# Sample attentions in four 32-column tiles, with contiguous cache runs, in a one-core decoder layer

## The chip, the core and the metric

The program runs on one core of a Trainium2 chip. Its engines are PE (TensorE, matmuls), DVE (VectorE), ACT (ScalarE), POOL (GpSimd) and SP (SyncE, which computes nothing and issues most of the transfers). The metric is the device time of one execution in microseconds (us). All data is fp32. The profile shows an fp32 matmul as two records on PE, each with a weight load of its own on PEld; a transpose, which is a matmul against the identity, is one record.

## What is computed

The layer takes a prompt of 1024 tokens and 8 samples of 8 new tokens each. The two parts that the change touches belong to the samples. In the self attention a sample has a cache of 1024 positions with 8 heads of 64; in the cross attention it has 256 memory positions with 4 heads of 256. Cut to what matters:

```python
# self attention of a sample, per dilation group (window, dil); kk, vv = cache + new rows
idx = wb + t[:, None] - kidx[None, :] * dil
s = einsum('bthd,btkhd->bthk', q, kk[idx]) * Dh ** -0.5 - slope * kidx * dil
o = einsum('bthk,btkhd->bthd', exp(s - lse), vv[idx])      # groups merged by their denominators
# cross attention of a sample
s = einsum('bthd,bmhd->bhtm', q, cache_mem_k) * 256 ** -0.5
o = einsum('bhtm,bmhd->bthd', softmax(s), cache_mem_v)
```

The kernel merges the three dilation groups into one softmax: a bias table holds the penalty and the logarithm of how many groups hold a key. The order of the keys is free as long as keys, values and bias agree on it.

## The kernel before

The kernel is a list of phases. In each, every engine has its own code, and between phases PE, DVE, ACT and POOL meet at a barrier (`meet`), so a phase that ends earlier moves all that follows. SP runs through its transfers with waits on semaphores and is not held by the barrier except where it waits for a phase by name. Nothing schedules the work: the order on an engine is the order of the code.

**Phase "win", the self attention over the cache** (`win_load`, `win_tensor`, `win_scalar`, `win_vector`). The keys of a sample (2 MB) and its values (2 MB) each have two buffers, `kc` and `vc`. Position `t * 128 + p` lies in partition p, so a partition receives eight runs of 2 KB. SP loads both in one queue: a key load waits until the transposes of the sample two before are done, a value load until that buffer's values have been used; the first two value loads wait until the stores of the phase before have landed. PE turns the keys (`turn_k(b, p)`, L1315: for each of four head pairs p eight transposes, four into bank 0 that ACT copies out and four into bank 1 that DVE copies out, `take_k`, L1391, into `kT`), and takes the scores of sample b from `kT` (`scores`, L1329). The stationary operand `QX[:, p, b, :]` has 64 columns (8 heads x 8 tokens) with zeros for the heads outside the pair p; four matmuls over p accumulate each of the two 512-key chunks and the 64 new keys. An even sample fills output rows 0 to 63, an odd one rows 64 to 127. `turn_k` of the next sample is spread between the pairs. Per pair of samples DVE and ACT do one softmax on 128 rows x 1088 (`softmax`, L1433 to L1441, with the exponential on ACT, L1417); `turn_p` turns the weights into `wpt`; `values` (L1360) multiplies them with all 512 value columns, eight cached blocks and one of new values per sample, 64 output rows at a time; of the result each head uses only its own 64 columns. `take_values` copies bank 7 out, `turn_o` turns it, and `output` (L1451) picks the useful blocks with 16 small copies. A `values` runs after the scores of every odd sample from the third on, for the pair before.

**Phase "xsample", the cross attention over the memory cache** (`xsample_load`, `xsample_tensor`, `xsample_scalar`, `xsample_vector`). Keys and values of a sample are 1 MB each. `turn_k(b, q)` (L1674) does four transposes into one of two banks and ACT copies them out (L1731). The scores of sample b (L1686) go to the 32-column tile `(0, 32 * i)` with i = b % 4: eight matmuls of 256 columns accumulate there, with a `turn_k` of the next sample after every second. After four samples (a quad) follow softmax, `values` (L1707: per sample four matmuls of 512 columns, all in the tile of that sample), the copy out (L1745), eight transposes (L1712) and the copies into `xhi` and `xlo`. SP loads the keys two samples ahead; the values of samples 0 to 3 are issued behind the keys of samples 0 and 1, those of 4 to 7 after all keys and once the buffer is free.

## Time and profile before

| what | value |
|---|---|
| median of three runs | 2445.07 us (2442.49 to 2447.41) |
| the profiled execution | 2447.53 us |
| its span in the trace | 2445.9 us |
| phase "win" | about 816 to 1005 us of the span |
| phase "xsample" | about 1404 to 1495 us of the span |
| PE busy, whole span | 2166.6 us (89%) |

The profile has a page with sums and the trace has the instructions with their start times. A time such as 904.90 is in us from the start of the span. The busy time of a matmul record includes its way through the array, so records that follow each other overlap in the trace; what PE needs per record is the distance between starts. "Idle before, releaser" names what an engine waited for; "issue" is time in which nothing visible held it.

### The profile page before, as it was taken

How to read it: one execution, taken by the hardware profiler on the slowest of the kernel's cores; microseconds unless marked ns; L12 is line 12 of the kernel's file. 1: busy time of each engine (PE TensorE's matmuls, PEld its weight loads, DVE VectorE, ACT ScalarE, POOL GpSimd, SP SyncE). 2: the span in 40 equal slices, each digit the busy share in tenths (PEclk: the TensorE clock that was granted, in tenths of full speed). 3: DMA queues.
4: the chain of work that ended last, by engine and by line, in shares of the span. 5: the costliest groups of instructions: out<-in, count | busy, mean ns of one | idle time of the engine just before them, and what ended most of it. 6: DMA issues, size and time to landing. Idle time of an engine off the chain costs nothing.

```text
span 2445.9 us, 29363 instructions
## 1 busy us (share of the span) xinstructions
PE 2166.6 (89%) x12542; PEld 1955.7 (80%) x12542; DVE 948.6 (39%) x1711; ACT 429.6 (18%) x759; POOL 70.2 (3%) x82
## 2 busy tenths in 40 slices
PE   6997997999377799498899788989999999999995
PEld 5995777999266544198898735989999999999995
DVE  7322442246665422444722301353333333333344
ACT  2004552001311121322201321030000000000013
POOL 3001000000021000000000000000000000000000
PEclk9998998999688799799999998999999999999997
DMA  5204331110053553311420042111111111111111
GB/s 174 61 17 168 130 121 36 43 43 17 15 190 138 181 200 120 138 56 45 138 69 35 4 181 99 43 43 43 32 54 44 39 40 51 43 41 52 41 30 73
DMA packets 181441, 188.94 MB, mean 77 GB/s; under 512 B 15879, under 2 KB 153639, under 8 KB 180586
## 3 DMA queue, kind: packets, MB, share of 16 engines
q1 hardware_dynamic: 180970, 170.97, 21.4%
q10 hardware_dynamic: 384, 16.78, 1.8%
q8 instruction: 59, 0.97, 0.2%
q14 instruction: 28, 0.23, 0.0%
HBM read 170.95 MB, written 50.33 MB: 90 GB/s over the span
## 4 chain that ended last, share of the span: by engine, by line
PE 47%; DVE 2%; ACT 2%; DMA 1%; issue 1%; DVEq 0%; ACTq 0%
PE psum L252 41%; PE psum L1560 1%; PE psum L1686 1%; PE psum L1707 1%; PE psum L1674 1%; ACT scratch L1581 1%; DVEq L182 0%; DMA weights_work<-in_cache_mem_k_dram 0%; DVE weights_lo L209 0%; DVE scratch L1618 0%; PE psum L1549 0%; DVE weights_hi L207 0%; PE psum L300 0%; DMA out_y_p_dram<-wide 0%; DMA weights_raw<-in_w_cv_dram 0%
## 5 line engine op out<-in xcount | busy, mean ns | idle before, releaser
L252 PE MATMUL psum<-x_hi,weights_hi 128*128 128x384 f32 (+1 forms) x2328 | 521.7, 332 | 43.5 <-DVE x_lo L290 18.9
L252 PE MATMUL psum<-x_lo,weights_hi 128*128 128x384 f32 (+1 forms) x2328 | 517.6, 330 | 0.0
L252 PE MATMUL psum<-x_hi,weights_lo 128*128 128x384 f32 (+1 forms) x2328 | 517.1, 330 | 0.0
L252 PEld LDWEIGHTS psum<-x_hi,weights_hi 128*128 128x128 f32 x2328 | 402.0, 190 | 49.1 <-issue 40.7
L207 DVE CAST weights_hi<-weights_raw 128x1024 fp32r<-128x1024 f32 (+2 forms) x144 | 94.6, 657 | 844.4 <-PE psum L252 830.8
L252 PEld LDWEIGHTS psum<-x_lo,weights_hi 128*128 128x128 f32 x2328 | 401.7, 190 | 0.0
L252 PEld LDWEIGHTS psum<-x_hi,weights_lo 128*128 128x128 f32 x2328 | 401.5, 189 | 0.0
L209 DVE TENSOR_TENSOR weights_lo<-weights_raw,weights_hi 128x1024 fp32r<-128x1024 f32 (+2 forms) x144 | 165.9, 1152 | 4.9
L252 PE MATMUL psum<-hidden_hi,weights_hi 128*128 128x384 f32 x528 | 117.2, 330 | 2.0 <-DVE hidden_lo L1822 2.0
L252 PE MATMUL psum<-hidden_lo,weights_hi 128*128 128x384 f32 x528 | 116.8, 329 | 0.0
L252 PE MATMUL psum<-hidden_hi,weights_lo 128*128 128x384 f32 x528 | 116.8, 329 | 0.0
L1795 ACT ACTIVATE scratch<-scratch 128x1088 f32<-128x1088 f32 x22 | 24.5, 1113 | 419.5 <-DVE scratch L1809 419.5
L252 PEld LDWEIGHTS psum<-hidden_hi,weights_hi 128*128 128x128 f32 x528 | 90.8, 189 | 2.2 <-DVE hidden_lo L1822 2.2
L252 PEld LDWEIGHTS psum<-hidden_lo,weights_hi 128*128 128x128 f32 x528 | 90.7, 189 | 0.0
L252 PEld LDWEIGHTS psum<-hidden_hi,weights_lo 128*128 128x128 f32 x528 | 90.6, 188 | 0.0
L567 PE MATMUL psum<-wide 128*128 128x512 f32 (+2 forms) x192 | 77.5, 514 | 1.9 <-ACTq L182 1.9
L618 DVE CUSTOM_DVE_ANT_0 scratch<-psum,weights_work 128x128 f32<-128x128 f32 (+3 forms) x64 | 48.5, 758 | 64.3 <-PE psum L567 41.6
L1797 ACT ACTIVATE hidden_hi<-scratch 128x1088 fp32r<-128x1088 f32 x22 | 24.5, 1114 | 269.0 <-DVE scratch L1820 269.0
L241 DVE TENSOR_TENSOR residual_T<-psum,residual_T 128x384 f32<-128x384 f32 x144 | 67.8, 527 | 5.7 <-PE psum L252 5.6
L579 PEld LDWEIGHTS psum<-ident,scratch 128*128 128x128 f32 x288 | 33.6, 142 | 43.1 <-ACT scratch L642 30.5
L1329 PE MATMUL psum<-wide,sample_q_wide 128*64 128x512 f32 x128 | 61.9, 607 | 4.4 <-DVE small L1438 2.7
L642 ACT ACTIVATE scratch<-scratch,small 128x128 f32<-128x128 f32 (+3 forms) x64 | 49.5, 774 | 92.1 <-DVE small L621 92.0
(295 smaller groups left out, 2245.5 us busy)
## 6 DMA issues: line engine op xcount, KB each, us to landing
work<-in_cache_win_k_dram SPq DMA_DIRECT2D x8, 2048.0 KB, 10.1
work<-in_cache_win_v_dram SPq DMA_DIRECT2D x8, 2048.0 KB, 9.7
weights_raw<-in_w_in_dram SPq DMA_DIRECT2D x28, 512.0 KB, 3.7
weights_raw<-in_w_gate_dram SPq DMA_DIRECT2D x22, 512.0 KB, 3.8
weights_raw<-in_w_up_dram SPq DMA_DIRECT2D x22, 512.0 KB, 3.7
weights_raw<-in_w_down_dram SPq DMA_DIRECT2D x24, 384.0 KB, 3.1
weights_work<-in_cache_mem_k_dram SPq DMA_DIRECT2D x8, 1024.0 KB, 5.0
wide<-in_cache_mem_v_dram SPq DMA_DIRECT2D x8, 1024.0 KB, 9.8
```

The lines of the kernel that those rows point to most:

```text
L207: nc.vector.tensor_copy(whi[:, w, 0:nk, :], raw[:, w, 0:nk, :]).then_inc(w_high, 1)
L209: nc.vector.tensor_tensor(wlo[:, w, 0:nk, :], raw[:, w, 0:nk, :], whi[:, w, 0:nk, :].bitcast(F32), ALU.subtract)\
L241: last = nc.vector.tensor_tensor(out, PS[:, 3 * ((n0 + j) % 2) + c, 0:w], out, ALU.add)
L252: mm = nc.tensor.matmul(PS[:, 3 * s + c, 0:n], w[:, s, k], x[part][:, k, t0:t0 + n], start=(k == 0 and w is whi and part == 0), stop=(k == ...
L567: mm = nc.tensor.matmul(PS[:, 2 * (u % 2) + g, 0:w], q_pad[:, h % 2, qb * P:(qb + 1) * P], ak[:, h // 2, 512 * g:512 * g + w], start=True, ...
L579: mm = nc.tensor.transpose(PS[:, 4 + n % 2, j * P:(j + 1) * P], logit[:, u % 3, (4 * g + j) * P:(4 * g + j + 1) * P], IDENT[:, :])
L618: chains["dve"](nc.vector.tensor_tensor_reduce(logit[:, u % 3, 0:w], PS[:, 2 * (u % 2):2 * (u % 2) + 2, :].rearrange("p a b -> p (a b)")[: ...
L642: nc.scalar.activation(logit[:, u % 3, 0:w], logit[:, u % 3, 0:w], ACT.Exp, bias=negm[:, i:i + 1], accum_out=asum[:, i:i + 1]).then_inc(pr ...
L1329: mm = nc.tensor.matmul(PS[HD * e:HD * e + HD, 2 + c, 0:w], QX[:, p, b, :], x, start=(p == 0), stop=(p == NP - 1))
L1560: mm = nc.tensor.matmul(PS[:, 6 + i // 4, (i % 4) * P:(i % 4 + 1) * P], mv_tok[:, m, i * P:(i + 1) * P], xpt[:, t % 2, (2 * h + m) * P:(2 ...
L1795: nc.scalar.activation(silu_g[:, q % 2], silu_g[:, q % 2], ACT.Silu).then_inc(silu_done, 1)
L1797: nc.scalar.activation(ghi[:, i], silu_g[:, q % 2], ACT.Copy).then_inc(h_high, 1)
```

## The change

Both sample attentions now spread each step over the four 32-column tiles of the array, with consecutive matmuls in different tiles.

- Self attention, scores: tile p holds head pair p, with 32 columns (2 samples x 2 heads x 8 tokens). `QX` has zeros for the other sample, and the two samples of a pair accumulate into the same rows. For each chunk of keys the four tiles take one matmul each. The transposes of the next sample follow the first chunk, the second chunk and, twice, the new keys.
- Self attention, values: tile p multiplies its 32 columns of weights with only the 128 value columns of its two heads. A sample has 36 matmuls of 128 columns where it had 9 of 512. The result is 256 columns wide for a pair of samples, so the copy out is half as wide, `turn_o` has two transposes for four, and `output` four copies for 16.
- Cross attention: tile h holds head h with the 32 rows of a quad. Scores of a sample are two groups of four matmuls, each followed by two `turn_k`; values are eight matmuls of 256 columns per sample.
- All four loads of cached keys and values give partition p the positions `p * n` to `p * n + n - 1`, one contiguous run of 16 KB (self) or 8 KB (cross). The bias table is permuted alike.
- The cached values of the self attention are issued by ACT, in `win_scalar`; SP keeps the keys, one after the other.

The core of the diff:

```diff
-        QX = sb("sample_q_wide", P, NP, DB, NS)
+        QX = sb("sample_q_wide", P, NP, DB, 32)
-                         A["cache_win_k"][b].rearrange("(t p) h d -> p t (h d)", p=P)).then_inc(kc_landed[b % 2], 16)
+                         A["cache_win_k"][b].rearrange("(p t) h d -> p t (h d)", p=P)).then_inc(kc_landed[b % 2], 16)
...
-            for pair in range(DB // 2):
-                if pair + 1 < DB // 2:
-                    load_k(sp, 2 * pair + 2)
-                if pair == 0:
-                    sp.wait_ge(out_stored, 16 * mark["state"])
-                    load_v(0)
-                    load_v(1)
-                if pair + 1 < DB // 2:
-                    load_k(sp, 2 * pair + 3)
-                if pair:
-                    load_v(2 * pair)
-                    load_v(2 * pair + 1)
+            for b in range(2, DB):
+                load_k(sp, b)
...
-                for p in range(NP):
-                    for c, (w, x) in enumerate(((512, k[:, p, 0:512]), (512, k[:, p, 512:PAST]), (NS, KNEW[:, p, :]))):
-                        mm = nc.tensor.matmul(PS[HD * e:HD * e + HD, 2 + c, 0:w], QX[:, p, b, :], x,
-                                              start=(p == 0), stop=(p == NP - 1))
-                    if p == NP - 1:
+                for c, w in enumerate((512, 512, NS)):
+                    for p in range(NP):
+                        x = KNEW[:, p, :] if c == 2 else k[:, p, 512 * c:512 * c + 512]
+                        mm = nc.tensor.matmul(PS[32 * p:32 * p + 32, 2 + c, 0:w], QX[:, p, b, :], x,
+                                              start=(e == 0), stop=(e == 1), tile_position=(0, 32 * p))
+                    if c == 2:
                         mm.then_inc(ws_ready, 1)
                     if b + 1 < DB:
-                        turn_k(b + 1, p)
+                        turn_k(b + 1, c)
+                if b + 1 < DB:
+                    turn_k(b + 1, 3)
...
-                    cs = slice(HD * e, HD * e + HD)
                     for t in range(KT + 1):
-                        p, v = (wpt[:, t, cs], vb[:, t, :]) if t < KT else (wpt[0:NS, t, cs], VNEW[:, :])
-                        mm = nc.tensor.matmul(PS[cs, 7, :], p, v, start=(t == 0), stop=(t == KT))
+                        for p in range(NP):
+                            rows = slice(32 * p, 32 * p + 32)
+                            w, v = (wpt[:, t, rows], vb[:, t, p * P:(p + 1) * P]) if t < KT else \
+                                (wpt[0:NS, t, rows], VNEW[:, p * P:(p + 1) * P])
+                            mm = nc.tensor.matmul(PS[rows, 7, e * P:(e + 1) * P], w, v, start=(t == 0), stop=(t == KT),
+                                                  tile_position=(0, 32 * p))
...
                 if b + 1 < DB:
                     take_k(act, 0, b + 1)
+                if b == 0:
+                    act.wait_ge(out_stored, 16 * mark["state"])
+                    load_v(act, 0)
+                    load_v(act, 1)
...
                     nc.scalar.activation(wl[:, :], wl[:, :], ACT.Exp, bias=negm[:, 0:1], accum_out=asum[:, 0:1]).then_inc(wl_free, 1)
+                    if b >= 3:
+                        act.wait_ge(wo_ready, b - 2)
+                        load_v(act, b - 1)
+                        act.wait_ge(wo_ready, b - 1)
+                        load_v(act, b)
...
-                    for k in range(KB):
-                        mm = nc.tensor.matmul(PS[32 * i:32 * i + 32, 2, 0:NMEM], cqx[:, k, b, :], ckT[b % 2][:, k, :],
-                                              start=(k == 0), stop=(k == KB - 1), tile_position=(0, 32 * i))
+                    for half in range(2):
+                        for h in range(XH):
+                            mm = nc.tensor.matmul(PS[32 * h:32 * h + 32, 2, 0:NMEM], cqx[:, 2 * h + half, b, :],
+                                                  ckT[b % 2][:, 2 * h + half, :], start=(i == 0 and half == 0),
+                                                  stop=(i == 3 and half == 1), tile_position=(0, 32 * h))
...
-                        if k % 2 and b + 1 < DB:
-                            turn_k(b + 1, k // 2)
+                        if b + 1 < DB:
+                            turn_k(b + 1, 2 * half)
+                            turn_k(b + 1, 2 * half + 1)
...
-                    for half in range(2):
-                        for m in range(2):
-                            mm = nc.tensor.matmul(PS[rows, 4 + half, :], ypt[:, m, rows], vb[:, m, 512 * half:512 * half + 512],
-                                                  start=(m == 0), stop=(m == 1), tile_position=(0, 32 * i))
+                    c0 = (i % 2) * XD
+                    for m in range(2):
+                        for h in range(XH):
+                            rows = slice(32 * h, 32 * h + 32)
+                            mm = nc.tensor.matmul(PS[rows, 4 + i // 2, c0:c0 + XD], ypt[:, m, rows], vb[:, m, h * XD:(h + 1) * XD],
+                                                  start=(m == 0), stop=(m == 1), tile_position=(0, 32 * h))
```

What stands in a row on the engines changes at three places. PE in the phase "win", from the first transposes on (L1315 is now L1305, L1329 now L1320; `128x128` is a transpose, the shape is output rows x moving columns). Before:

```order
L1315 MATMUL psum<-ident,work_55 128x128 x32
L1329 MATMUL psum<-wide,sample_q_wide 64x512 x2
L1329 MATMUL psum<-sample_k_new,sample_q_wide 64x64
L1315 MATMUL psum<-ident,work_55 128x128 x8
L1329 MATMUL psum<-wide,sample_q_wide 64x512 x2
```

After:

```order
L1305 MATMUL psum<-ident,work_55 128x128 x32
L1320 MATMUL psum<-wide,sample_q_wide 32x512 x4
L1305 MATMUL psum<-ident,work_55 128x128 x8
L1320 MATMUL psum<-wide,sample_q_wide 32x512 x4
L1305 MATMUL psum<-ident,work_55 128x128 x8
L1320 MATMUL psum<-sample_k_new,sample_q_wide 32x64 x4
L1305 MATMUL psum<-ident,work_55 128x128 x16
```

A sample had four alternations of scores and transposes; it has three, with the last 16 transposes in a row.

PE at the values of one pair in the same phase (L1360 is now L1355). Before:

```order
L1360 MATMUL psum<-work_54,scratch 64x512 x8
L1360 MATMUL psum<-sample_v_new,scratch 64x512
```

After:

```order
L1355 MATMUL psum<-work_54,scratch 32x128 x32
L1355 MATMUL psum<-sample_v_new,scratch 32x128 x4
L1355 MATMUL psum<-work_54,scratch 32x128 x32
```

Each sample has four times as many matmuls, each a quarter as long in moving columns.

ACT in the same phase, where the value loads (`work_54`) now stand among its copies and exponentials (L1391 is now L1387). After, from the start of the phase:

```order
L1387 ACTIVATE wide<-psum 128x512 x8
L1292 DMA work_54<-in_cache_win_v_dram 128x4096 x2
L1387 ACTIVATE wide<-psum 128x512 x4
L1417 ACTIVATE scratch,small<-scratch,small 128x1088
L1387 ACTIVATE wide<-psum 128x512 x4
L1398 ACTIVATE scratch<-psum 128x512 x2
L1400 ACTIVATE scratch<-psum 64x128
L1387 ACTIVATE wide<-psum 128x512 x4
L1417 ACTIVATE scratch,small<-scratch,small 128x1088
L1292 DMA work_54<-in_cache_win_v_dram 128x4096 x2
```

SP before, at the same place, had keys and values in one queue:

```order
L1274 DMA work_55<-in_cache_win_k_dram 128x8x512
L1291 DMA work_54<-in_cache_win_v_dram 128x8x512 x2
L1274 DMA work_55<-in_cache_win_k_dram 128x8x512 x3
L1291 DMA work_54<-in_cache_win_v_dram 128x8x512 x2
```

It now holds six key loads in a row, and the values come from ACT.

PE in the phase "xsample", from the first scores on (L1686 is now L1691, L1674 now L1678). Before:

```order
L1686 MATMUL psum<-wide,cross_sample_q 32x256 x2
L1674 MATMUL psum<-ident,weights_work 128x128 x4
```

After:

```order
L1691 MATMUL psum<-wide,cross_sample_q 32x256 x4
L1678 MATMUL psum<-ident,weights_work 128x128 x8
```

A sample had four such alternations, and has two.

## Rows read from the trace of the kernel before

**Rows 1.** Busy time by stretch, both phases: us, PE, PEld, DVE, ACT, POOL, clock, DMA, GB/s.
```profile
816.00:1005.00 189.00, 171.40 (x644) 77.22 (x644) 38.91 (x129) 31.31 (x57) 0.00 (x0) 0.97 0.52 177
1404.00:1495.10 91.10, 76.65 (x340) 34.22 (x340) 2.86 (x15) 23.78 (x49) 0.00 (x0) 0.93 0.43 162
```
**Rows 2.** Timeline of PE, one quarter of a sample's scores: start, us, what, records.
```profile
904.90 1.93 PE L1329 MATMUL psum<-wide,sample_q_wide 128*64 128x512 f32 x4
906.67 0.28 PE L1329 MATMUL psum<-sample_k_new,sample_q_wide 128*64 128x64 f32 x2
906.87 1.09 PE L1315 MATMUL psum<-ident,work 128*128 128x128 f32 x8
907.90 1.93 PE L1329 MATMUL psum<-wide,sample_q_wide 128*64 128x512 f32 x4
```
**Rows 3.** Timeline of PE, the values of one sample.
```profile
927.85 7.08 PE L1360 MATMUL psum<-work,scratch 128*64 128x512 f32 x16
934.86 1.07 PE L1360 MATMUL psum<-sample_v_new,scratch 64*64 64x512 f32 x2
935.86 7.08 PE L1360 MATMUL psum<-work,scratch 128*64 128x512 f32 x16
```
**Rows 4.** Timelines of PE and PEld where column tiles change (L1707, then L1329 to L1360).
```profile
1443.98 8.86 PE L1707 MATMUL psum<-wide,scratch 128*32 128x512 f32 x32 [0.47 <-ACT scratch L1743]
1445.73 0.14 PEld L1707 LDWEIGHTS psum<-wide,scratch 128*32 128x32 f32 x3 [0.32 <-issue]
...
964.24 0.64 PE L1360 MATMUL psum<-work,scratch 128*64 128x512 f32 x1
964.66 0.59 PE L1329 MATMUL psum<-wide,sample_q_wide 128*64 128x512 f32 x1
964.72 0.59 PE L1360 MATMUL psum<-work,scratch 128*64 128x512 f32 x1
```
**Rows 5.** Timeline of DVE: copies of turned keys with nothing else between.
```profile
821.55 0.69 DVE L1391 COPY wide<-psum 128x512 f32<-128x512 f32 x1 [0.76 <-PE psum L1315]
822.99 0.69 DVE L1391 COPY wide<-psum 128x512 f32<-128x512 f32 x1 [0.75 <-PE psum L1315]
```
**Rows 6.** Timeline of PE: waits for the softmax, and for keys and values from memory.
```profile
845.23 1.97 PE L1315 MATMUL psum<-ident,work 128*128 128x128 f32 x8 [5.76 <-DMA work<-in_cache_win_k_dram]
859.38 1.90 PE L1329 MATMUL psum<-wide,sample_q_wide 128*64 128x512 f32 x4 [2.67 <-DVE small L1438]
984.11 8.75 PE L1360 MATMUL psum<-work,scratch 128*64 128x512 f32 x16 [1.77 <-issue]
```
**Rows 7.** Timeline of SP: issue of the self attention's keys of sample 2.
```profile
835.48 0.41 SPq L1274 DMA_DIRECT2D work<-in_cache_win_k_dram  x1
```
**Rows 8.** Page, part 6: issues, size of one, median us from issue to landing.
```profile
work<-in_cache_win_k_dram SPq DMA_DIRECT2D x8, 2048.0 KB, 10.1
weights_work<-in_cache_mem_k_dram SPq DMA_DIRECT2D x8, 1024.0 KB, 5.0
residual_T<-residual_T_dram SPq DMA_DIRECT2D x1, 4352.0 KB, 13.5
```
**Rows 9.** Busy time by stretch, while loads stand in a queue (columns as Rows 1).
```profile
845.00:862.00 17.00, 13.50 (x56) 7.28 (x56) 5.41 (x12) 3.68 (x6) 0.00 (x0) 0.91 1.05 386
1464.00:1475.00 11.00, 10.31 (x54) 5.05 (x53) 0.00 (x0) 3.86 (x7) 0.00 (x0) 1.00 1.02 413
```
**Rows 10.** The chain that ended last, in the phase "xsample": start, us, what.
```profile
1407.75 11.48 DMA weights_work<-in_cache_mem_k_dram
...
1433.73 0.60 PE psum L1674 x4
1434.35 0.61 ACT wide L1731
1435.00 1.05 PE psum L1686 x4
...
1482.32 10.54 PE psum L1707 x32
```

More of the change, by code:

```diff
@@ L53, in constants @@
     t = np.arange(DT)
-    cache = np.stack(bias(PAST + t[:, None] - np.arange(PAST)[None])).reshape(AW // DT, PAST)
-    new = np.stack(bias(t[:, None] - t[None])).reshape(H * DT, DT)
-    sample_new = np.full((2, H * DT, DB // 2, DB, DT), NEG)
-    for pair in range(DB // 2):
-        for e in range(2):
-            sample_new[e, :, pair, 2 * pair + e] = new
+    key = np.arange(PAST).reshape(P, -1).T.ravel()
+    rows = lambda x: np.broadcast_to(x.reshape(NP, 1, 2, DT, -1), (NP, 2, 2, DT, x.shape[-1])).reshape(P, -1)
+    cache = rows(np.stack(bias(PAST + t[:, None] - key[None])))
+    new = rows(np.stack(bias(t[:, None] - t[None])))
+    sample_new = np.full((P, DB // 2, DB, DT), NEG)
+    for r in range(P):
+        for pair in range(DB // 2):
+            sample_new[r, pair, 2 * pair + r // 16 % 2] = new[r]
     s = np.arange(P)
@@ L517, in q_wide_pool @@
                 rows = slice(HD * e, HD * e + HD)
[L518 to L521 removed]
+                for odd in range(2):
+                    c0 = 16 * odd + DT * e
+                    chains["pool"](nc.gpsimd.tensor_copy(QX[rows, :, odd::2, c0:c0 + DT],
+                                                         aq[rows, :, SEQ:N].rearrange("p j (b t) -> p j b t", t=DT)[:, :, odd::2]))
             chains["pool"](nc.gpsimd.tensor_copy(KNEW[:, :, :], ak[:, :, SEQ:N]))
@@ L1256, in build @@
         kT = cut(HB, BIG, NP, PAST), cut(HB, BIG + 4096, NP, PAST)
[L1257 removed]
+        wo = cut(HB, BIG + 8192, 2, 2 * P)
         vc = cut(XN, 0, 2, KT * AW)
@@ L1364, in turn_o @@
                 pe.wait_ge(wv_taken, pair + 1)
-                for j in range(NP):
-                    mm = nc.tensor.transpose(PS[:, 7, j * P:(j + 1) * P], wo[:, pair % 2, j * P:(j + 1) * P], IDENT[:, :])
+                for e in range(2):
+                    mm = nc.tensor.transpose(PS[:, 7, e * P:(e + 1) * P], wo[:, pair % 2, e * P:(e + 1) * P], IDENT[:, :])
                 mm.then_inc(wo_turned, 1)
@@ L1407, in take_values @@
                 act.wait_ge(wo_ready, 2 * pair + 2)
-                nc.scalar.activation(wo[:, pair % 2, :], PS[:, 7, :], ACT.Copy).then_inc(wv_taken, 1)
+                nc.scalar.activation(wo[:, pair % 2, :], PS[:, 7, 0:2 * P], ACT.Copy).then_inc(wv_taken, 1)
             take_k(act, 0, 0)
@@ L1448, in output @@
                         rows = slice(HD * r, HD * r + HD)
-                        for j in range(NP):
-                            h = 2 * j + r
-                            last = nc.vector.tensor_copy(cat[rows, j, SEQ + b * DT:SEQ + (b + 1) * DT],
-                                                         PS[rows, 7, j * P + HD * e + DT * h:j * P + HD * e + DT * (h + 1)])
+                        c0 = 16 * e + DT * r
+                        src = PS[rows, 7, e * P:(e + 1) * P].rearrange("p (j c) -> p j c", j=NP)[:, :, c0:c0 + DT]
+                        last = nc.vector.tensor_copy(cat[rows, 0:NP, SEQ + b * DT:SEQ + (b + 1) * DT], src)
                 last.then_inc(wo_taken, 1)
@@ L1657, in xsample_pool @@
             chains["pool"](nc.gpsimd.memset(cqx[:, :, :, :], 0.0))
-            for h in range(XH):
-                for k in (2 * h, 2 * h + 1):
-                    last = nc.gpsimd.tensor_copy(cqx[:, k, :, h * DT:(h + 1) * DT], cq[:, k, SEQ:N].rearrange("p (b t) -> p b t", t=DT))
+            for b in range(DB):
+                i = b % 4
+                last = nc.gpsimd.tensor_copy(cqx[:, :, b, i * DT:(i + 1) * DT], cq[:, :, SEQ + b * DT:SEQ + (b + 1) * DT])
             last.then_inc(cqx_ready, 1)
```

27 lines of the change are left out of this document (9 added, 18 removed).

## The prediction

> **What bounds the kernel now.** I read the busy time by stretch first, since the phases are separated by barriers and the change touches two of them. In both, PE is the busy engine: 171 of 189 us in "win" and 77 of 91 us in "xsample" [rows 1]; DVE and ACT are under a third, the transfers at about half. So PE's order of work is the clock of both phases, with a few waits in between. The timeline of PE shows what it is made of. A quarter of a sample's scores in "win" is four records of 512 columns (904.90 to 906.67, so 1.77 us, 0.43 us plus a switch), two of 64 columns (0.20 us) and eight transposes (906.87 to 907.90, 1.03 us): 3.00 us, 12.0 us per sample [rows 2]. The values of a sample take 8.01 us, from 927.85 to 935.86, of which the cached blocks are 7.01 us at 0.44 us a record [rows 3]. In "xsample" a quarter is 0.98 us of scores and 0.59 us of transposes, with 0.65 us for the last copy before the next sample's scores [rows 10]: 4 x 1.57 + 0.7, so 7.0 us per sample.
>
> **What four tiles are worth.** The question that decides this case is whether matmuls in different column tiles run side by side. The trace has three places where it shows. L1707 goes through its 32-column tiles one after the other, eight records each; its 32 records would take 13.7 us at 0.43 us, and they took 8.86 [rows 4]. The gap is the tile changes: the last four records of a tile run beside the first four of the next, which gives 5 x 4 x 0.43 = 8.6 us. At 964.24 to 964.72 the same is seen between 64-column tiles of two different steps, each stream still at its own pace of 0.43 to 0.48 us [rows 4]. In both cases the newcomer started when three unstarted records stood before it. In the new order two records of a tile alternate with two of the next, so the fourth tile's first record has exactly three unstarted before it: all four tiles can run at once. Weight loads do not stand against it for long streams: three 32-column loads began and ended within 0.14 us while one takes 0.11 [rows 4]. Two tiles at a time are shown, four are not; that is where the bounds come from.
>
> The row comes first here, because the Trainium skill speaks against it (TensorE: Matmul & The Clock Gate, Part 3, on what overlaps): it says weight loads overlap running matmuls only when the row group differs, and that matmuls keep strict order. All tiles here use the same rows, so by that rule nothing would overlap; that is the third rival below. The trace does not agree, since 8.86 us is less than 13.7.
>
> **The change, "win" scores.** For each 512-key chunk, eight records in four tiles: 2 x 0.43 + three starts of 0.03 = 0.95 us if all four run, plus the eight transposes, 1.03, and 0.1 for the switches: 2.1 us. New keys: eight short records, about 0.25 (bounds 0.2 and 0.8, four times the 0.20 of [rows 2]), with eight transposes 1.4. The last eight transposes follow directly and are held by the copies of ACT and DVE, whose pace with nothing else between is 1.44 us per head pair [rows 5]. Sum 2.1 + 2.1 + 1.4 + 1.45 = 7.1 us for 12.0, so 4.9 us for seven samples; the last sample has no transposes and goes from 7.3 to 2.0. Together 39.6 us. Copies, softmax and the turned weights stay as they are.
>
> **"win" values.** 72 records per sample: 64 of 128 columns. A transposing record with as many columns goes at (1.03 / 8) 0.13 us with its switches, 0.11 without; four at once make 64 x 0.11 / 4 = 1.8 us, plus 0.3 for the new values: 2.1. If only one runs at a time it is 7.3 + 0.5 = 7.8 (no gain at all), with two 4.3. Short records in four tiles are nowhere in the trace; I take 2.6, near the fast end, because the streams of [rows 4] did not slow each other, but not at it. That is 5.4 us off 8.01 for each of 8 samples: 43 us. Two transposes for four and four copies for 16: 1.5 us in all.
>
> **"win" loads.** A gain in PE's time hits the loads next, so I follow the phase in time. SP issues the keys of sample 2 (K2) at 835.48, behind the state stores, which do not move [rows 7]. Landing times: 5.0 us for 1024 KB and 13.5 for 4352 KB [rows 8], a slope of 2.55 us per MB and 2.4 fixed, so 7.6 us for 2 MB in long runs against 10.1 now. In a queue, 2 KB runs moved 386 GB/s and 4 KB runs 413 [rows 9]; longer runs I put at 430 (bounds 390 and 440). Now K2 stands before the values in one queue; after, ACT issues V0 beside it. No row shows two queues. K2 lands at 843 if it goes first, 847 if it shares; I take 847. PE reaches this wait at 834 and idles 13 us where it idled 5.8 [rows 6]. From there: rest of sample 1 and the softmax's reading, 856 (2.5 us are waited as now 2.67 [rows 6]); K3 lands at 857; sample 2 and the turned weights of pair 0 to 865; sample 3 and values to 877; sample 4 to 886; sample 5 and values to 899; sample 6 to 908; sample 7 to 910; first values of pair 2 to 912.4, which lets V6 be issued, landing at 920; V7 right behind, 925. PE waits for both, about 5 us together, and ends its values at 927.6; with copy, transposes and outputs 929.7. After the two long waits PE runs at half clock for some us: the transposes at 845.23 took 1.97 us for 1.09, the values at 984.11 8.75 for 7.08 [rows 2, 3, 6]. I add 3: the phase ends at 933 for 1005, **72 us** earlier. The same by parts: 39.6 + 43 + 1.5, less 10 of new waits and 3 of clock, is 71. ACT's waits on `wo_ready` hold only its copies for the sample after, which PE has not begun by then; two issues cost it under 1 us each time. With 390 GB/s the end is 2.5 us later.
>
> The Trainium skill (DMA: Bandwidth & Descriptors, "Issuing engines are not separate DMA queues") says that transfers of different issuers run on the same 16 engines and interleave. By it K2 shares and 847 stands; without it the phase would end some 4 us earlier. No row before shows it.
>
> **"xsample".** Per sample two groups of eight records of 256 columns: 2 x 0.22 + 0.1, eight transposes 1.0, switches 0.1: 1.65 each; then the last copy 0.65 and about 0.4 because ACT's four copies (0.6 each and a handover of 0.17) become the pace: 4.4 us for 7.0. K2 lands where it does now, at 1419.2, because SP issues it behind four value loads [rows 10]; so what samples 0 and 1 gain, PE waits. From 1419: rest of sample 1 with half clock 6 us, sample 2 4.4, sample 3 to the start of the values 6.5, values 3.6 (64 records of 256 columns in four tiles, 16 x 0.22) for 8.9, copy and transposes 2.2: 1441.8. Quad 1: three samples to 1455, scores and softmax 4.1; but the last key load and the four value loads, 5.2 MB, are issued at 1445.5 and take 14.3 us as now, so the values start at 1459.8. They are again at half clock at first (10.54 for 8.86 us now [rows 4, 10]): 5 us. Copies and transposes 2.2: 1467 for 1495.1, **28 us** earlier. POOL builds both wide queries off the path, in as many or fewer copies.
>
> **Sum.** 2447.5 - 72 - 28 = 2347.5 against the profiled execution, which lay 2.5 above the median: **2345 us**.
>
> **Rivals.** (1) *Half the overlap*: two tiles at a time, or short records held by their weight loads. "win": 8.9 us per sample and 4.3 per values, end at 953 (52 us off); "xsample" 18 us off. 2375 us. For it: two is what is shown. Against it: nothing slowed when two ran. (2) *The loads bound it*: with all waits as forecast but 14 loads of 2 MB at 390 and no overlap of issue and landing (7.6 to 10.1 us for each lone load, as now), each of three pairs gives back about 5 us: 2360; inside the range. (3) *No overlap when tiles alternate*: scores as now, 8 x 0.43 per chunk; values in "win" 7.8 for 8.0; but the values of "xsample" lose the overlap they have, 13.8 for 8.9 and 10.5, so +8; shorter runs of switches -5, contiguous loads -2: 2448, no change. (4) *Slower*: an alternating record waits until the one before has left the array. A record's 0.59 us against its pace of 0.43 gives 0.16 us each [rows 3, 4]; over 576 value records, 192 score records and 256 in "xsample" that is 165 us beyond (3), 2610. It decides from the point where overlap is worth less than one stream; the records at 964.72 contradict it.
>
> **How the numbers follow.** Forecast, all four tiles, 2322 to 2362 with the loads' bounds: 0.62. Rival 1, 2362 to 2392: 0.25. Rival 3: 0.05. Rival 4 and anything that makes it longer: 0.04. The rest, 0.04, is between rivals 1 and 3 (2392 to 2440). Range 2322 to 2392 holds 0.87. Under 0.2% (5 us) a measurement of this kernel cannot tell from no change. Faster 0.91, same 0.05, slower 0.04.
>
> **What would show it.** Right: scores in "win" start in four tiles within 0.1 us and the next four 0.43 us later; a sample takes about 7 us; values 2 to 3 us; waits for K2 near 847 and for V6 and V7; the phases about 117 and 63 us long. Wrong: starts of different tiles 0.43 us apart (rival 3) or in twos (rival 1); records longer than 0.59 us; values near 4 us; K2 landing at 843 or after 850; PE at half clock through the short stretches, whose price is up to 8 us for a phase.

## The result, and the profile after

The changed kernel takes **2341.62 us**, the median of four runs (2341.15 to 2344.16); the kernel before took 2444.49 beside it. The ratio is 0.958, with a 95% interval of 0.9564 to 0.9597: 103 us less. The forecast was 2345 us.

The profiled execution after took 2344.16 us, with a span of 2342.3. The first view to read is again the busy time by stretch, in the columns of [rows 1]. The rows are the whole phase "win", the whole phase "xsample", the 10 and the 20 us from 839.00 (PE waits for the keys of sample 2 from 835.23 to 846.14, and then works), and a stretch at the start of the cross attention's first values:

```profile
818.80:929.70 110.90, 86.56 (x1068) 56.09 (x1068) 35.54 (x80) 30.54 (x57) 0.00 (x0) 0.88 0.78 302
1328.50:1393.00 64.50, 41.60 (x404) 25.00 (x404) 2.76 (x14) 22.31 (x49) 0.00 (x0) 0.84 0.57 229
839.00:849.00 10.00, 2.86 (x16) 1.77 (x16) 0.69 (x1) 0.60 (x1) 0.00 (x0) 0.51 1.01 433
839.00:859.00 20.00, 10.04 (x60) 5.47 (x61) 5.41 (x12) 3.68 (x6) 0.00 (x0) 0.68 1.01 431
1358.10:1361.40 3.30, 2.83 (x30) 1.30 (x32) 0.00 (x0) 0.38 (x1) 0.00 (x0) 0.50 0.59 248
```

"win" is 110.9 us long for 188.8, "xsample" 64.4 for 90.9: 77.9 and 26.5 us, 104.4 together, which is the whole gain (the rest of the layer moved by about 1 us the other way). PE executes more matmul records than before (1068 for 644 in "win") in half the busy time (86.6 us for 171.4), because four of them run at once. The share of transfers rose from 0.52 to 0.78: they are now the next thing that PE meets. The granted clock fell from 0.97 to 0.88 in "win", and reads 0.51 from 839.00 to 849.00, where PE mostly waits for K2.

The timeline of PE after, one sample's scores from first record to last, in the columns of [rows 2]:

```profile
877.67 1.07 PE L1320 MATMUL psum<-wide,sample_q_wide 128*32 128x512 f32 x8
878.66 1.09 PE L1305 MATMUL psum<-ident,work 128*128 128x128 f32 x8
879.69 1.06 PE L1320 MATMUL psum<-wide,sample_q_wide 128*32 128x512 f32 x8
...
881.71 0.32 PE L1320 MATMUL psum<-sample_k_new,sample_q_wide 128*32 128x64 f32 x8
882.03 1.19 PE L1305 MATMUL psum<-ident,work 128*128 128x128 f32 x8
883.37 1.29 PE L1305 MATMUL psum<-ident,work 128*128 128x128 f32 x8
884.50 1.04 PE L1337 MATMUL psum<-ident,scratch 128*128 128x128 f32 x8
```

Eight records of 512 columns take 0.99 us until the next group starts (877.67 to 878.66), where four took 1.77 [rows 2]; the sample goes from 877.67 to 884.50, 6.83 us for 12.0. In the trace's single records the four tiles start 7 ns apart and the same tile's next record 0.43 us later: four streams at one stream's pace. The values are the clearest place:

```profile
873.20 1.95 PE L1355 MATMUL psum<-work,scratch 128*32 128x128 f32 x64
875.08 0.42 PE L1355 MATMUL psum<-sample_v_new,scratch 64*32 64x128 f32 x8
875.43 1.95 PE L1355 MATMUL psum<-work,scratch 128*32 128x128 f32 x64
```

64 records of 128 columns take 1.88 us (873.20 to 875.08), a sample's values 2.23, for 8.01 [rows 3]. A round of four starts every 0.109 us in single records.

Then the waits, which answer to [rows 6]; here the timeline of PE at the places where "win" waits for memory or for the softmax:

```profile
846.14 1.97 PE L1305 MATMUL psum<-ident,work 128*128 128x128 f32 x8 [10.91 <-DMA work<-in_cache_win_k_dram]
856.36 1.94 PE L1320 MATMUL psum<-wide,sample_q_wide 128*32 128x512 f32 x8 [2.67 <-DVE small L1443]
918.83 3.64 PE L1355 MATMUL psum<-work,scratch 128*32 128x128 f32 x64 [4.39 <-DMA work<-in_cache_win_v_dram]
923.62 3.64 PE L1355 MATMUL psum<-work,scratch 128*32 128x128 f32 x64 [0.56 <-DMA work<-in_cache_win_v_dram]
```

PE waits 10.91 us for K2 where it waited 5.76, and 4.39 and 0.56 us for V6 and V7, where it waited 1.77 us for V6 alone. After each of these waits the records take almost twice their time: eight transposes 1.97 us for 1.09, the values 3.64 for 1.95. The granted clock reads 0.51 there, that is 1.2 and not 2.4 GHz. In all, "win" holds 27 us at the lower level: 3.4 at its start, and from 839.2 for 10.2 us, from 856.3 for 3.4 and from 917.7 for 10.2. Before it held 12, of which 4.9 at its start. The clock column says the same: 0.88 of 110.9 us and 0.97 of 189.

In "xsample" the same views show the wait for its K2, the first values, a sample (from 1365.89 to 1369.88, 3.99 us for 7.0 [rows 10]) and the last values:

```profile
1343.30 1.97 PE L1678 MATMUL psum<-ident,weights_work 128*128 128x128 f32 x8 [6.87 <-DMA weights_work<-in_cache_mem_k_dram]
1358.73 4.99 PE L1715 MATMUL psum<-wide,scratch 128*32 128x256 f32 x64 [0.47 <-ACT scratch L1751]
...
1365.89 0.64 PE L1691 MATMUL psum<-wide,cross_sample_q 128*32 128x256 f32 x8
...
1369.88 0.64 PE L1691 MATMUL psum<-wide,cross_sample_q 128*32 128x256 f32 x8 [0.74 <-ACT wide L1739]
...
1385.35 5.33 PE L1715 MATMUL psum<-wide,scratch 128*32 128x256 f32 x64 [4.24 <-issue]
```

And SP's queue, where the loads of those phases are issued (K2 in "win", the last four values in "xsample", the first load of the phase after):

```profile
835.93 49.09 SPq L1276 DMA_DIRECT2D work<-in_cache_win_k_dram  x6
...
1369.55 2.08 SPq L1656 DMA_DIRECT2D wide<-in_cache_mem_v_dram  x4
1392.94 1.00 SPq L201 DMA_DIRECT2D weights_raw<-in_w_co_dram  x2
```

### The profile page after: what moved, and what is told of

Read it like the earlier page. It is cut to its first block, busy times and chain, and to the rows that moved or that the text cites. A ratio compares the mean times of both kernels' runs of the same rounds, so it can differ in the third digit from the quotient of the medians.

```text
span 2342.3 us, 30287 instructions
## 1 busy us (share of the span) xinstructions
PE 2049.9 (88%) x13030; PEld 1928.3 (82%) x13030; DVE 945.5 (40%) x1663; ACT 427.6 (18%) x759; POOL 68.7 (3%) x78
## 4 chain that ended last, share of the span: by engine, by line
PE 48%; DVE 2%; ACT 2%; DMA 1%; issue 1%; DVEq 1%; ACTq 0%
PE psum L254 43%; PE psum L1564 1%; ACT scratch L1585 1%; PE psum L1678 1%; DMA weights_work<-in_cache_mem_k_dram 1%; DVEq L184 0%; DVE weights_lo L211 0%; PE psum L1715 0%; DVE scratch L1622 0%; PE psum L1553 0%; PE psum L1691 0%; DVE weights_hi L209 0%; PE psum L302 0%; ACT wide L1739 0%; PE psum L1843 0%
## 5 line engine op out<-in xcount | busy, mean ns | idle before, releaser
L277 ACT ACTIVATE scratch<-residual_T 128x1088 f32<-128x1088 f32 x24 | 26.7, 1114 | 212.8 <-DVE residual_T L243 212.8
```

The costliest lines, as they stand in the source:

```text
L277: nc.scalar.activation(nsq[:, (j0 + k) % 2, 0:cols], src[:, k, 0:cols], ACT.Square).then_inc(sq_ready, 1)
```

## The experiments

The theory: the gain is four column tiles running at once, cut by the waits for K2, V6 and V7 and by the lower clock behind them. The other two parts of the change (contiguous runs, values issued by ACT) are worth little in it. The rivals: the layout of the loads carries it; ACT's issues cost or gain nothing; the wait for K2 is only a matter of when it is issued. All times are medians, each beside runs of the kernel before on the same chip. The kernel before took 2444.49 to 2447.66 us from one group of runs to the next, and the changed kernel itself was run again only beside e9 and e10. So where e4, e5, e7 and e8 are compared with the changed kernel, a difference of medians is uncertain by some 3 us, and the length of a phase in the profiled execution says more: two profiled executions of the changed kernel have 110.9 and 111.0 us in "win", 64.4 and 65.4 in "xsample".

| run | what it is | us | ratio to before, 95% |
|---|---|---|---|
| e1 | self attention's part alone | 2370.04 | 0.9697 (0.9679 to 0.9714) |
| e2 | cross attention's part alone | 2420.74 | 0.9909 (0.9886 to 0.9932) |
| e3 | longer runs of records in one tile | 2357.79 | one run |
| e4 | SP issues the values | 2355.58 | 0.9631 (0.9612 to 0.9649) |
| e5 | short runs in the loads | 2355.13 | 0.9629 (0.9609 to 0.9650) |
| e6 | before, with contiguous runs | 2442.71 | 0.9986 (0.9977 to 0.9996) |
| e7 | K2 issued earlier | 2337.50 | 0.9553 (0.9537 to 0.9569) |
| e8 | cross values issued earlier | 2339.69 | 0.9553 (0.9531 to 0.9575) |
| e9 | e7, with V0 and V1 later | 2336.70 | 0.9555 (0.9532 to 0.9578) |
| e10 | e9 and e8 together | 2329.34 | 0.9514 (0.9495 to 0.9534) |
| e11 | the changed kernel, beside e9 and e10 | 2345.54 | 0.9579 (0.9556 to 0.9602) |

### One part alone

e1 undoes the cross attention's part, e2 the self attention's. The core of e1's edit against the changed kernel, the scores and the values:

```diff
-                    for half in range(2):
-                        for h in range(XH):
-                            mm = nc.tensor.matmul(PS[32 * h:32 * h + 32, 2, 0:NMEM], cqx[:, 2 * h + half, b, :],
...
+                    for k in range(KB):
+                        mm = nc.tensor.matmul(PS[32 * i:32 * i + 32, 2, 0:NMEM], cqx[:, k, b, :], ckT[b % 2][:, k, :],
...
-                        for h in range(XH):
-                            rows = slice(32 * h, 32 * h + 32)
...
+                    rows = slice(32 * i, 32 * i + 32)
```

> The change in the self attention alone; the cross attention's scores, values and loads as before. Theory (tiles run side by side, and phases add through the barriers): the phase win is as in the changed kernel, 75 us shorter than before, xsample keeps its 91 us; about 2370 us, ratio 0.969 to 0.971. Rival (the two parts share something, such as code length, clock or transfers, so that they do not add): over 5 us away from 2370.

> The change in the cross attention alone. Theory: xsample takes 64 to 65 us where it took 91, win keeps its 189; about 2418 us, ratio 0.989. With the self-attention-only kernel the two gains sum to 103 us. Rival (not additive): sum under 95 or over 110.

e1 takes 2370.04 us: 75.8 us of the gain, with "win" 110.2 us long and "xsample" 90.9 as before. e2 takes 2420.74: 25.1 us, with "win" 188.6 and "xsample" 64.1. The two add up to 101 of 103 us, as expected: the parts do not touch each other, as phases behind barriers should not.

### How many records of one tile may stand in a row

The prediction read from [rows 4] that a record of another tile starts once at most three unstarted ones stand before it. That gives a number for every order of the 64 value records. e3 gives each pair of samples another order, in runs of 16, 8, 4 and 2 records a tile (a group of `g` blocks is two records a block):

```diff
-                    for t in range(KT + 1):
-                        for p in range(NP):
+                    g = (8, 4, 2, 1)[pair]
+                    for t, p in [(t, p) for t0 in range(0, KT, g) for p in range(NP) for t in range(t0, t0 + g)] + [(KT, p) for p in range(NP)]:
```

> The changed kernel, where the matmuls of the self attention's cached values are ordered in runs per tile: 8 matmuls (16 records) in a tile before the next tile in the first pair of samples, 4 (8 records) in the second, 2 (4 records) in the third, 1 (2 records) in the last pair as in the changed kernel. Theory (a record in another tile can start while three unstarted records stand before it, not more): per sample, with 0.109 us a record and 0.35 for the new values, 16 records a run give 4 x 12 x 0.109 + 0.44 + 0.35 = 6.0 us; 8 give 4.3; 4 give 2.2, as fast as 2. Rival A (tiles overlap however they are ordered): 2.2 us in all. Rival B (only direct neighbours overlap): 4 records a run give 5.7, 8 give 6.7, 16 give 7.2. In total up to 10 us slower than the changed kernel by the theory, less what the waits for keys and values take up.

The timeline of PE of e3, one sample of each pair:

```profile
875.67 5.95 PE L1355 MATMUL psum<-work,scratch 128*32 128x128 f32 x64
881.56 0.42 PE L1355 MATMUL psum<-sample_v_new,scratch 64*32 64x128 f32 x8
...
903.63 4.33 PE L1355 MATMUL psum<-work,scratch 128*32 128x128 f32 x64
907.89 0.42 PE L1355 MATMUL psum<-sample_v_new,scratch 64*32 64x128 f32 x8
...
923.26 2.00 PE L1355 MATMUL psum<-work,scratch 128*32 128x128 f32 x64
925.19 0.42 PE L1355 MATMUL psum<-sample_v_new,scratch 64*32 64x128 f32 x8
...
938.92 1.95 PE L1355 MATMUL psum<-work,scratch 128*32 128x128 f32 x64 [0.60 <-DMA work<-in_cache_win_v_dram]
```

The same 64 records take 5.89 us in runs of 16 (875.67 to 881.56), 4.26 in runs of 8, 1.93 in runs of 4 and 1.88 in runs of 2. With 0.35 for the new values that is 6.24, 4.61 and 2.28 where the theory had 6.0, 4.3 and 2.2; an order that made no difference would have shown 2.2 in all of them, one that paid for every change another row of numbers. So the overlap hangs on the order of the code, and a short look ahead: up to four records of one tile in a row it is nearly full, at eight about half of it is gone (4.26 us, between 1.88 and the 7.01 of [rows 3]). Two tiles only were not tried. The whole took 2357.79 us in its one execution, with "win" 122.4 us long for 110.9, where up to 10 us more were expected: by the theory's own numbers the two slow pairs cost 2 x 3.8 + 2 x 2.1 = 11.8 us, by the measured ones 12.8.

### The values issued by SP

e4 lets SP issue the values in the old kernel's order, and takes the issues out of ACT's code; tiles and runs stay as changed:

```diff
         def win_load(sp):
-            for b in range(2, DB):
-                load_k(sp, b)
+            for pair in range(DB // 2):
+                if pair + 1 < DB // 2:
+                    load_k(sp, 2 * pair + 2)
+                if pair == 0:
+                    sp.wait_ge(out_stored, 16 * mark["state"])
+                    load_v(sp, 0)
+                    load_v(sp, 1)
+                if pair + 1 < DB // 2:
+                    load_k(sp, 2 * pair + 3)
+                if pair:
+                    for b in (2 * pair, 2 * pair + 1):
+                        sp.wait_ge(wo_ready, b - 1)
+                        load_v(sp, b)
```

> The changed kernel with the cached values of the self attention issued by SP again, in the order of before (K2, V0, V1, K3, ...). Theory (two queues share the 16 engines, K2 loses by it): K2 lands about 4 us earlier, PE waits 7 us for it where it waits 10.9, but K3 comes behind both values, about 857 to 858, where PE would want it at 853, so that most is given back: total within 4 us of the changed kernel, 2338 to 2346. Rival 1 (issuing on ACT is what brings a gain): over 5 us slower than the changed kernel. Rival 2 (K2 does not lose by sharing): K2 lands as in the changed kernel, 10.2 us after its issue.

It takes 2355.58 us, 14 more than the changed kernel, with "win" 122.8 us long for 110.9, 12 more. The expectation of at most 4 us missed, and its rival held. The timelines of e4, first PE's waits for keys, then SP's issues:

```profile
841.04 1.97 PE L1316 MATMUL psum<-ident,work 128*128 128x128 f32 x8 [8.13 <-DMA work<-in_cache_win_k_dram]
856.75 1.97 PE L1316 MATMUL psum<-ident,work 128*128 128x128 f32 x8 [3.55 <-DMA work<-in_cache_win_k_dram]
...
894.57 1.97 PE L1316 MATMUL psum<-ident,work 128*128 128x128 f32 x8 [6.98 <-DMA work<-in_cache_win_k_dram]
```
```profile
833.22 0.36 SPq L1276 DMA_DIRECT2D work<-in_cache_win_k_dram  x1
...
875.86 2.56 SPq L1303 DMA_DIRECT2D work<-in_cache_win_v_dram  x2
878.47 6.85 SPq L1276 DMA_DIRECT2D work<-in_cache_win_k_dram  x2
```

K2 lands sooner when the values stand behind it in its own queue: PE turns it 7.8 us after its issue (833.22 to 841.04), in the changed kernel 10.2 after (835.93 to 846.14). V0 is issued 0.86 us after K2 in both, here by SP behind K2 (834.08), there by ACT (836.79); so it is the second issuer, and not a later start, that makes the two share. That part of the prediction holds. But K3 now stands behind V0 and V1 (3.55 us of waiting), and K6 is issued only at 878.47, behind V2 and V3, whose waits on `wo_ready` SP has to sit out: 6.98 us. With one issuer and this order the keys wait for values that nobody needs yet. In the changed kernel the two streams wait apart, and against the old order in one list that is worth 12 us ("win") to 14 (medians). A better order in SP's one list (K3 ahead of V0, K6 and K7 ahead of V2) was not tried; how much of this needs a second issuer is not shown.

### Short runs in the loads

e5 turns the layout of the cache loads back (each partition takes its rows one by one) in both phases, with the bias in the matching order of keys; e6 puts contiguous runs into the kernel before:

```diff
-    key = np.arange(PAST).reshape(P, -1).T.ravel()
+    key = np.arange(PAST)
...
-                         A["cache_win_k"][b].rearrange("(p t) h d -> p t (h d)", p=P)).then_inc(kc_landed[b % 2], 16)
+                         A["cache_win_k"][b].rearrange("(t p) h d -> p t (h d)", p=P)).then_inc(kc_landed[b % 2], 16)
```

> The changed kernel with the cache positions spread over the partitions as before (runs of 2 KB in the self attention, 4 KB in the cross attention), the bias in its old order. Theory (the loads' rate matters only where PE waits for them): 386 for 430 GB/s and a slower start of each load make the waits for K2, V6 and V7 and for the cross values longer by 1 to 2 us each, 3 to 8 us in all: 2345 to 2350. Rival 1 (a large part of the gain is from the contiguous runs): 20 us or more slower. Rival 2 (they bring nothing): within 2 us of the changed kernel.

> The kernel before, with contiguous cache runs as the only change. Theory (PE is the clock of both phases there, loads show in waits of 5.8, 1.1, 1.8 and 2.8 us): 2 to 5 us faster, 2440 to 2442. Rival (long runs are a large part of the change): 15 us or more faster.

e5 takes 2355.13 us, 13.5 more than the changed kernel; 3 to 8 were expected, so this missed upwards. e6 takes 2442.71, 3.6 us less than the kernel before (ten runs; 0.9977 to 0.9996, so 1 to 6 us), inside the 2 to 5 expected. In its profiled execution "win" is 182.6 us long for 188.8, 6 us less, so this number is not sharp. The layout alone is worth some 4 us by the medians and 7 by the two phases, beside the tiles 12 to 14 ("win" and "xsample" together grow by 13.5 in e5). The timeline of PE of e5 shows where, and its busy time by stretch the rate (columns of [rows 1]):

```profile
827.07 1.09 PE L1305 MATMUL psum<-ident,work 128*128 128x128 f32 x8 [1.53 <-DMA work<-in_cache_win_k_dram]
...
847.24 1.97 PE L1305 MATMUL psum<-ident,work 128*128 128x128 f32 x8 [12.24 <-DMA work<-in_cache_win_k_dram]
...
901.83 3.64 PE L1355 MATMUL psum<-work,scratch 128*32 128x128 f32 x64 [4.48 <-DMA work<-in_cache_win_v_dram]
...
929.28 3.64 PE L1355 MATMUL psum<-work,scratch 128*32 128x128 f32 x64 [5.99 <-DMA work<-in_cache_win_v_dram]
```
```profile
838.00:858.00 20.00, 8.23 (x48) 5.08 (x48) 4.35 (x10) 2.39 (x4) 0.00 (x0) 0.66 1.03 370
```

370 GB/s stand against 431 in the same place of the changed kernel. The waits for K2, V6 and V7 are 1.3, 1.6 and 0.4 us longer, and there are new ones of 1.53 us for K1 and 4.48 for V3: 9.3 us of the 13.5. Behind each of those over 4 us the work runs at half clock (3.64 us for 1.95). Slower transfers cost PE the time and then the clock. "win" is 123.4 us long for 110.9, "xsample" 65.5 for 64.4.

### Taking the waits away

K2 stands behind the state stores in SP's queue, though its buffer is free earlier. e7 lets ACT issue it as soon as it has copied the last keys of sample 0:

```diff
         def win_load(sp):
-            for b in range(2, DB):
+            for b in range(3, DB):
                 load_k(sp, b)
...
             take_k(act, 0, 0)
+            load_k(act, 2)
```

> The changed kernel, where ACT issues the load of K2 once the first sample's keys are turned (about 824), ahead of the state stores' end, instead of SP behind them (835.9). Theory (PE's wait of 10.9 us for K2 and the half clock behind it are exposed, and the state stores are what holds K2): K2 lands by 837 at the latest, the wait shrinks to under 2 us, the phase win is 8 to 13 us shorter; 2329 to 2334 us. Rival (the next load, K3, or the store traffic of small packets takes its place): less than 4 us gained.

It takes 2337.50 us, 4 less than the changed kernel (6 by the ratios), and "win" is 105.8 us long for 110.9, 5 less, where 8 to 13 were expected. The wait for K2 to land is gone, and another stands after its first eight transposes. The timelines of e7, PE and then ACT:

```profile
840.58 1.97 PE L1305 MATMUL psum<-ident,work 128*128 128x128 f32 x8 [4.13 <-ACT wide L1387]
```
```profile
838.74 1.09 ACTq L1292 DMA_DIRECT2D work<-in_cache_win_v_dram  x2
839.92 0.60 ACT L1387 ACTIVATE wide<-psum 128x512 f32<-128x512 f32 x1 [7.57 <-issue]
```

Before its half of the copies of K2, ACT waits until the state stores have left the buffers of V0 and V1, 7.57 us, issues these two at 838.74, and only then copies. In the changed kernel the same wait cost nothing, since K2 was late anyway: the prediction, which let ACT's waits on `wo_ready` cost nothing and did not speak of this one, was right only under that cover. e9 therefore also moves V0 and V1 one step down ACT's list:

```diff
-                if b == 0:
+                if b == 1:
                     act.wait_ge(out_stored, 16 * mark["state"])
```

> The changed kernel with K2 issued early by ACT, and V0 and V1 issued by ACT one sample later, after its copies of K2. Theory (with K2 early, ACT's wait for the state stores, which stands ahead of its copies of K2, held PE 4.1 us and brought the half clock; that wait now comes after those copies): no wait of PE between 834 and the softmax, the phase win 10 to 13 us shorter than in the changed kernel, and the total 8 to 13 us below it. Rival (K3, behind the state stores at about 838, takes its place at once): under 6 us.

> The changed kernel itself, on the same chip as the two others, to compare with: 2340 to 2345 us, ratio 0.958.

e9 takes 2336.70 us, the changed kernel beside it (e11) 2345.54, just above the 2340 to 2345 expected: 8.8 us, inside the 8 to 13, though single runs of the two meet (2342.62 and 2342.20). "win" is 101.8 us long for 111.0 in e11, 9.3 less where 10 to 13 were expected. The timeline of PE of e9 shows the softmax's 2.67 us as the first wait that is left, and then a short one for K3:

```profile
840.61 1.94 PE L1320 MATMUL psum<-wide,sample_q_wide 128*32 128x512 f32 x8 [2.67 <-DVE small L1444]
```
```profile
845.08 1.97 PE L1305 MATMUL psum<-ident,work 128*128 128x128 f32 x8 [2.54 <-DMA work<-in_cache_win_k_dram]
```

So the rival of e9, K3 in the place of K2, holds in a small part. The lower clock is there too: the records behind the softmax's wait take 1.94 us for 1.06.

e11 also shows how far one profile can be read. It is the changed kernel again, and its timeline of PE has the first values of "xsample" at full clock, 3.66 us for the 4.99 of the first profile:

```profile
1363.16 3.66 PE L1715 MATMUL psum<-wide,scratch 128*32 128x256 f32 x64 [0.47 <-ACT scratch L1751]
```

Its half clock around the wait for K2 lasts longer instead, 13.7 us for 10.2 (0.50 from 1341.8 to 1355.3), and its "xsample" is 65.4 us long for 64.4.

In "xsample" the values V4 to V7 stand behind the last key load. e8 issues V4 and V5 ahead of it:

```diff
...
+                if b == DB - 1:
+                    load_v(4)
+                    load_v(5)
                     sp.wait_ge(yk_turned, 4 * (b - 1))
                 sp.dma_start(ck[:, b % 2, :].rearrange("p (t n) -> p t n", n=D), kd[b]).then_inc(ck_landed[b % 2], 16)
...
+            load_v(6)
+            load_v(7)
```

> The changed kernel, where the cross attention's values of samples 4 and 5 are issued ahead of the last keys instead of behind them. Theory (PE's wait of 4.2 us before the second quad's values, and the half clock after it, come from these loads standing behind the last keys): the wait goes down to under 1 us, 4 to 6 us gained, 2336 to 2338 us. Rival (the last keys, now behind 2 MB more, make PE wait as long for them): within 2 us of the changed kernel.

"xsample" is 60.7 us long for 64.4, 3.7 less where 4 to 6 were expected. The 4.24 us of PE in front of the last values are 0.47, as the timeline of PE of e8 has it; the values themselves still take 5.35 us, at half clock:

```profile
1380.17 5.35 PE L1722 MATMUL psum<-wide,scratch 128*32 128x256 f32 x64 [0.47 <-ACT scratch L1758]
```

So the half clock of these values does not need that wait, from which e8 had expected it to come: waits of 1.73 us for the softmax and 0.47 for a copy stand ahead of them, and the clock fell all the same.

The whole kernel took 2339.69 us, where 2336 to 2338 were expected; 2 us less than the changed kernel is within what such runs differ by, so what e8 says rests on the length of its phase. e10 has both edits:

> The same, with the cross attention's values of samples 4 and 5 ahead of the last keys as well. Theory (barriers make the two gains add): 4 to 5 us below the kernel with the early K2 alone, 12 to 17 below the changed kernel.

e10 takes **2329.34 us** (2327.19 to 2331.16), 16.2 less than e11 and 7.4 less than e9, and is faster than the kernel before and the changed one: 0.9514 (0.9495 to 0.9534). Its phases are 101.9 and 60.9 us long. The 16.2 us lie within the 12 to 17 expected; the 7.4 over e9 are more than the 4 to 5 expected, and the phase "xsample" explains 3.8 of them (60.9 us for 64.7 in e9); the rest is spread between runs. What is left for PE to wait for in "win" is above all K3 and V6, in its timeline:

```profile
848.73 1.97 PE L1305 MATMUL psum<-ident,work 128*128 128x128 f32 x8 [3.59 <-DMA work<-in_cache_win_k_dram]
...
910.89 3.64 PE L1355 MATMUL psum<-work,scratch 128*32 128x128 f32 x64 [4.17 <-DMA work<-in_cache_win_v_dram]
```

A third buffer for values might answer the wait for V6; it was not tried. The longest wait left is in "xsample": 6.93 us for its K2, which is issued behind four value loads that PE needs only later. No run moved it.

## Why the prediction held, point by point

- **Four tiles run at once.** Right, and the step that decided. It was read from two tiles in [rows 4]; e3 bears out the reading with three more orders. The Trainium skill (TensorE: Matmul & The Clock Gate, Part 3) has weight loads overlap matmuls only if the row group differs. The trace does not agree: all four tiles use the same rows, and start 7 ns apart. But the prediction concluded too much from it when it said that by the section nothing would overlap: the section's own table of measured speedups gives three 32-column tiles 2.38 times. Four gave a sample's values 3.6 times here (8.01 to 2.23 us).
- **Scores in "win", 7.1 us a sample.** 6.83 measured, and 1.85 for the last sample where 2.0 was said. Together 41.6 us for 39.6.
- **Values in "win", 2.6 us.** 2.23 measured: the fast bound was 2.1, and the caution of 0.5 us was not needed. 46.2 us for 43.
- **K2 at 847, V6 and V7 about 5 us.** 846.14, and 4.39 and 0.56. PE waited 10.9 us for K2, not 13. All waits for memory in "win" grew by 6.6 us, from 9.2 (0.64, 5.76, 1.05 and 1.77) to 15.9, for 10 foreseen. The sharing of the queues was read right: 10.2 us from issue to use beside V0 and V1, 7.8 with K2 ahead of them (e4). The Trainium skill (DMA: Bandwidth & Descriptors, "Issuing engines are not separate DMA queues") says that transfers interleave whoever issues them; these two numbers agree.
- **The clock, 3 us in "win".** The parts give 41.6 + 46.2 + 1.5 = 89.3, less 6.6 of waits is 82.7; 77.9 were measured. So 4.8 us are the clock's and what no view assigns, for 3. The time at 1.2 GHz rose by 15, from 12 to 27 us; it costs less than half of that, because in part of it PE waits.
- **"win" 72 us.** 77.9: against the 71 of the sum by parts, scores (2.0), values (3.2) and waits (3.4) each came out a little better than said, the clock (1.8) a little worse.
- **"xsample" 28 us.** 26.5, and two terms failed. *Values of quad 0, 3.6 us:* 4.99, because PE was at half clock from 1358.1 to 1361.5 (0.50); the prediction had put the half clock at quad 1 only, where it also stood (5.33). The wait for K2 is not its direct cause, since PE was back at full clock from 1347.8 to 1358.1; shorter waits of 0.74 and 1.78 us stand before it. In e11 the same values took 3.66 us, so this term is one execution's: which step meets the lower clock changes from run to run, and why is open. *The last values 14.3 us after their issue:* 15.8 (1369.55 to 1385.35). The last of the four loads, issued at 1371.18, landed 14.1 us later; 14.3 was right for that load, but the prediction counted it from the first issue, and the issues take over 2 us. This wait took back what a sample gained more than said (3.99 us for 4.4). K2 of this phase was turned 14.8 us after the phase's start, as before (15.1): there the gain of samples 0 and 1 did become waiting.
- **Contiguous runs, 2.5 us.** The prediction put 430 GB/s into its sum, and 431 were measured, so the sum stood. Its price for a lower rate, 2.5 us at 390 GB/s, looks too small: at 370 it was 12 to 14 us (e5), since new waits appear and the long ones send PE to half clock.
- **ACT's issues cost nothing.** True for the changed kernel and incomplete: the prediction never asked what the alternative cost, which is 12 to 14 us in the old order (e4), nor saw that ACT's wait is covered by K2's lateness alone (e7).
- **The total.** 2341.6 for 2345: scores, values and waits of "win" were each better than said by 2.0 to 3.4 us, its clock 1.8 and "xsample" 1.5 worse. The mechanism was right; that the total is off by 3.4 us only is in part luck, since these go both ways.
- **The rivals.** Half the overlap (2375), the bound by loads (2360), no overlap (2448) and a drain per record (2610) all fall by the rows of 873.20 and 877.67. The loads' rival was nearest in kind: e4 and e5 sit at 2355, where a queue or a rate is a little worse.

## What to carry to other kernels

Where stationary operands are 32 columns wide, alternate the four column tiles every few records, instead of finishing one tile first: the same 64 records took 5.89 us in runs of 16 and 1.88 in runs of 2. When PE gets that much faster, price every load again, by who issues it and what wait stands before it in that engine's list; keys and values with different waits should not block each other in one list. And count a wait of some microseconds twice, once as time and once as the clock of the work behind it.

## What the runs showed of the hardware

- Four 32-column tiles of fp32 matmuls run side by side without slowing: starts 7 ns apart, next round after 0.109 us (128 columns) or 0.43 us (512). A sample's values went 3.6 times faster.
- The overlap reaches over four records of one tile (1.93 us) and not over eight (4.26) or sixteen (5.89).
- Loads of 2 MB moved 370 to 386 GB/s in runs of 2 KB, 431 in runs of 16 KB, and two issuers share that rate: a load took 10.2 us from issue to use beside another issuer's, 7.8 ahead of the same loads in one queue.
- After a wait of 4 to 11 us PE was granted half the clock (0.50 to 0.51) for the work that followed: values in 3.64 us for 1.95, transposes in 1.97 for 1.09. After shorter waits (0.74 and 1.78 us) it sometimes was: the same values of "xsample" took 4.99 us in one execution of the changed kernel and 3.66 in another.
